# RWKV chunk inverse: the first product of each level as 64x64 blocks, one head at a time, the two lanes alternating between the halves of the array

## The reference, cut to what matters

```
def _rwkv7_step(S, inp):
    r_t, w_t, k_t, v_t, kk_t, b_t = inp
    sa = jnp.einsum('bhvk,bhk->bhv', S, -kk_t)
    S = S * w_t[:, :, None, :] + sa[..., None] * b_t[:, :, None, :] + v_t[..., None] * k_t[:, :, None, :]
    y = jnp.einsum('bhvk,bhk->bhv', S, r_t)
    return S, y
```

## Time and profile before

| | us |
|---|---|
| median of 3 runs | 4005.11 (3998.64 to 4005.95) |
| the profiled execution, its own time | 4005.71 |
| its span, first to last instruction | 4003.9 |
| PE busy in the span | 3716.2 (93%) |
| the chunk stage, first to last `lx` | 1157.1 to 1884.3 of the span |

### The profile page before, as it was taken

The page is one execution under the profiler, slowest core; times in us unless marked ns, Lnnn a source line. Parts: engine busy times, 40 slices in busy tenths (PEclk is TensorE's granted clock), DMA queues, the critical chain, the costliest instruction groups (busy, mean ns, idle before and its releaser), DMA issues. The chain is left out here.

```text
span 4003.9 us, 60255 instructions
## 1 busy us (share of the span) xinstructions
PE 3716.2 (93%) x23340; PEld 3513.3 (88%) x23340; DVE 1701.5 (42%) x2728; ACT 1095.0 (27%) x1680; POOL 77.9 (2%) x67
## 2 busy tenths in 40 slices
PE   6999999996659999999799797999999999799899
PEld 6999999995449999999799686999999999778687
DVE  6566622223856666666443445222222222211333
ACT  5211134334633333333311333111111111111211
POOL 0000000000010000100000000000000000000000
PEclk8999999997779999999899998999999999899999
DMA  5333343343642222221432441111111110311342
GB/s 146 98 117 113 114 143 118 124 126 124 231 134 49 53 58 54 47 54 30 143 114 93 151 138 55 53 52 42 42 42 53 51 42 32 115 51 50 110 124 92
DMA packets 316612, 357.97 MB, mean 89 GB/s; under 512 B 169024, under 2 KB 265152, under 8 KB 304752
## 3 DMA queue, kind: packets, MB, share of 16 engines
q1 hardware_dynamic: 316528, 356.83, 28.5%
HBM read 221.75 MB, written 135.00 MB: 89 GB/s over the span
## 5 line engine op out<-in xcount | busy, mean ns | idle before, releaser
L2225 PE MATMUL psum<-h_hi,up_w_hi 128*128 128x344 f32 x2112 | 676.6, 320 | 15.4 <-DVE up_w_lo L2269 15.4
L2225 PE MATMUL psum<-h_lo,up_w_hi 128*128 128x344 f32 x2112 | 677.6, 321 | 0.0
L2225 PE MATMUL psum<-h_hi,up_w_lo 128*128 128x344 f32 x2112 | 675.4, 320 | 0.0
L434 PE MATMUL psum<-x_hi,proj_w_hi 128*128 128x344 f32 x1632 | 535.0, 328 | 9.4 <-DVE proj_w_lo L521 8.4
L434 PE MATMUL psum<-x_lo,proj_w_hi 128*128 128x344 f32 x1632 | 524.9, 322 | 0.0
L434 PE MATMUL psum<-x_hi,proj_w_lo 128*128 128x344 f32 x1632 | 523.6, 321 | 0.0
L2225 PEld LDWEIGHTS psum<-h_hi,up_w_hi 128*128 128x128 f32 x2112 | 398.3, 189 | 15.5 <-issue 15.5
L2225 PEld LDWEIGHTS psum<-h_hi,up_w_lo 128*128 128x128 f32 x2112 | 398.5, 189 | 0.0
L2225 PEld LDWEIGHTS psum<-h_lo,up_w_hi 128*128 128x128 f32 x2112 | 397.8, 188 | 0.0
L434 PEld LDWEIGHTS psum<-x_hi,proj_w_hi 128*128 128x128 f32 x1632 | 309.3, 189 | 11.1 <-issue 8.5
L2019 PE MATMUL psum<-down_w_hi,down_a_hi 128*128 128x512 f32 x704 | 281.0, 399 | 39.7 <-DVE down_w_lo L2139 29.8
(11 more groups left out here) (305 smaller groups left out, 6236.6 us busy)
## 6 DMA issues: line engine op xcount, KB each, us to landing
up_weight<-in_w_up_tiles SPq DMA_DIRECT2D x22, 1024.0 KB, 4.8
scratch_hidden<-up_hidden SPq DMA_DIRECT2D x22, 1024.0 KB, 3.9
down_a_raw<-scratch_hidden SPq DMA_DIRECT2D x32, 704.0 KB, 5.1
proj_area<-scratch_s_tab SPq DMA_DIRECT2D x32, 608.5 KB, 3.8
scratch_s_tab<-proj_area SPq DMA_DIRECT2D x16, 1089.0 KB, 4.3
proj_weight<-in_w_in_tiles SPq DMA_DIRECT2D x34, 512.0 KB, 4.8
scratch_gates<-proj_mixed SPq DMA_DIRECT2D x16, 1032.0 KB, 4.4
scratch_rwkv_proj<-proj_mixed SPq DMA_DIRECT2D x14, 1032.0 KB, 6.2
```

The costliest lines, as they stand in the source:

```text
L434: mm = nc.tensor.matmul(psum[:, bank(v, n), 0:N_TOK], w[:, v, k, :], x[:, k, cols], start=(k == 0 and w is w_hi and x is x_hi), stop=(k == ...
L2225: mm = nc.tensor.matmul(psum[:, bank(u, part, n), 0:N_TOK], w[:, u, part, k, :], y[:, k, block_cols(n)], start=(k == 0 and w is w_hi and y ...
```

## The change

In each level, the first product is made for both lanes together instead of lane after lane. TensorE first waits for the inputs of both lanes, and then adds to a new semaphore `lx_begun`, for which nothing waits. Each matmul of 128x128 becomes two of 64x64, one for each head: the weights are the head's block of `l_t` (rows and columns of the head), the moving operand is 64 columns of `x` on the head's 64 partitions, and the result goes to the head's 64 partitions and 64 columns of the bank. The two blocks outside the diagonal are no longer written; they keep what the bank held, and the mask multiplies them by zero. In the order, lane 0 on one head alternates with lane 1 on the other: lane 0 head 0 pair 0, lane 1 head 1 pair 0, and so on over the pairs, then the same with the heads exchanged. The last matmul of each lane tells VectorE of it. Everything else stands as before.

```
@@ -1177,15 +1177,29 @@
-            def lx(lane, v, k, l):
+            def lx_inputs(lane, v, k, l):
                 if l == 0:
                     at(pe, x1_ready[lane], 1, k, 1)
                 else:
                     at(pe, x_ready[lane], LEVELS, k, l)
                     at(pe, xt_ready[lane], LEVELS - 1, k, l)
-                for j in range(PAIRS):
-                    mm = T_.matmul(bank(LX[lane])[:, j, :], l_t[:, lane, j, :], x[:, lane, j, :], start=True, stop=True)
-                mm.then_inc(lx_done[lane], 1)
+
+            def one_head(out, weights, moving, lane, j, h):
+
+                rows, block_ = slice(h * S, (h + 1) * S), slice(h * S, (h + 1) * S)
+                return T_.matmul(bank(out[lane])[rows, j, block_], weights[rows, lane, j, block_], moving[rows, lane, j, block_], start=True, stop=True)
+
+            def lx(place, l):
+                for lane in place:
+                    lx_inputs(*place[lane], l)
+                pe.sem_inc(lx_begun, 1)
+                for other in range(2):
+                    for j in range(PAIRS):
+                        for lane in place:
+                            h = other if lane == 0 else 1 - other
+                            mm = one_head(LX, l_t, x, lane, j, h)
+                            if other == 1 and j == PAIRS - 1:
+                                mm.then_inc(lx_done[lane], 1)
@@ -1297,7 +1311,9 @@
                     for chain in (lx, xq, turn_x):
-                        if l < count - 1 or chain is not turn_x:
+                        if chain is lx:
+                            lx(place, l)
+                        elif l < count - 1 or chain is not turn_x:
                             for lane in place:
```

More of the change, by code:

```diff
@@ L1009, in rwkv_chunks @@
     GROUPS = (NC_ + 1) // LANES
-    (masks_loaded, pre_loaded, a_loaded, r_loaded, cleared, bkv_cleared, main_cleared, late_cleared, grams_cleared, eps_set) = sems(name, [
-        "masks_loaded", ("pre_loaded", LANES), ("a_loaded", 4), ("r_loaded", 4), "cleared", "bkv_cleared", "main_cleared", "late_cleared", "grams_cleared", "eps_set"])
+    (masks_loaded, pre_loaded, a_loaded, r_loaded, lx_begun, cleared, bkv_cleared, main_cleared, late_cleared, grams_cleared, eps_set) = sems(name, [
+        "masks_loaded", ("pre_loaded", LANES), ("a_loaded", 4), ("r_loaded", 4), "lx_begun", "cleared", "bkv_cleared", "main_cleared", "late_cleared", "grams_cleared", "eps_set"])
     (grams_done, masked, q_init, toks_done, toks_ready, x1_turned, x1_ready, lx_done, q_ready, xq_done, x_ready, xt_turned, xt_ready) = sems(name + "_pre", [
```

## The result

| | us |
|---|---|
| before, median of 5 runs | 4000.38 (3998.64 to 4005.95) |
| changed, median of 5 runs | 4014.14 (4008.63 to 4022.21) |
| ratio, changed to before | 1.0033, 95% interval 1.0017 to 1.0049 |
| the profiled execution of the changed kernel, and its span | 4018.77, 4017.0 |

The span is 13.1 us longer than that of before.

A forecast was written before the change was run, and what follows sets the result against it. TensorE, busy 713.6 of 730 us in the chunk stage, was taken as the bound; -9.0 us over 16 groups and +0.6 for the first gave -8.4, so 3997 us, range 3985 to 4035.

The forecast's parts named there:

- rival B: Chunk-stage product: only every second pair of matmuls overlaps, product some 1.4 us deep, +20 us, 4025; chance 0.12.
- C: Chunk-stage product: no overlap, records one after another at 0.06 us, +3.7 us a group, 4066 (4081 at 0.066); chance 0.20.
- Two halves at once: First product: matmuls on different array halves overlap fully, 16 records deep at 0.06 us, 0.96 us.
- The passage between shapes: Into and out of the 64x64 blocks: next load unhidden, 0.20 us after the last record's start, 0.09 of it pause.
- Rival A: Passages to 64x64 and back need no pause and hide their loads: -0.96 us a group, -15 us, 3990; chance 0.10.
- The common wait: Before each product both lanes wait for ScalarE's second copy; first load 0.06 us after it, VectorE's first multiplication starts later.
- The increment of `lx_begun`: One sequencer instruction for each product, costed at nothing; without cover, below 0.05 us x 83.
- The sum for a group: Levels 0 to 4 give 0, +0.05, -0.47, +0.19, -0.33 us: -0.56 us a group, -9.0 us over 16 groups.
- the matmuls double to 32 records: First product of both lanes: 32 records, costed at 0.06 us each, 16 deep if two run at once.
- The first group: One-lane group, no alternation: smaller records and passages of 0.2 us cost +0.6 us over three levels.
- 16 records at 0.06 instead of 8 at 0.112: One-lane group's product: record count and pace in us, part of its +0.6 us over three levels.
- The clock in the stage: Chunk stage: granted clock still 1.00 after the change; a fall to the lower level would make all of this wrong.

The follow-up runs named there:

- the two after it: Changed product in levels 2 and 4 alone, ratio 1.0012 to the kernel before; in level 2 alone, 1.0016; both keep TensorE's two-group loop.

## Why the prediction was wrong, point by point

The forecast was 8.4 us less; the medians say 13.8 us more. That the time lies within the range is luck: the range reached to 4035 for rival B, half an overlap, and B is not what happened. The chance of 0.32 for a slower kernel stood on B and C alone.

- **Two halves at once: right.** 0.030 us a record for both streams together; the forecast had 0.06 in each. Rivals B and C are out. C leaned on the Trainium skill's rule in "TensorE: Matmul & The Clock Gate", part 1, of 62 ns of sequencer time for each matmul without hardware decoding. That case is not this one: 32 matmul records took 1.15 us, not the 1.98 that the prediction had from the rule.
- **The passage between shapes: right.** `xq` and the pieces start where the sum has them. In the changed kernel's level 3 the first load comes at 1523.88, 0.20 after the start of the last record before it, and the next load after the product is 1.11 later than its first, as forecast. Rival A is out: the loads are not hidden.
- **The common wait: right in place, a little off in size.** The load follows the end of ScalarE's second copy by 0.11 us (1509.46 + 1.08 to 1510.65), not 0.06. The increment of `lx_begun`, costed at nothing, is not what makes the difference: with one event instruction that carries both waits and the increment it is 0.07. How the waits are spread over the sequencer's instructions was not in the sum. Where they make two event instructions, as in the written-out kernel, that costs 0.54 us a group, as much as the whole gain. In the loop it cost little and did not turn the result.
- **The sum for a group: right.** -0.56 forecast, 44.55 against 45.12 measured with the loop written out and one event instruction. It is no luck of terms that cancel. From one product's first load to the next (levels 0 to 1, 1 to 2, 2 to 3, 3 to 4, and 4 to 0 of the next group) the forecast's starts and terms ask for -0.15, -0.09, -0.47, +0.34 and -0.19 us; that run against the written-out kernel before has -0.14, -0.08, -0.51, +0.34 and -0.18.
- **The step that failed: "the matmuls double to 32 records", costed as engine time only.** The instructions behind them were counted nowhere. 320 more in a body of 1685 (334 by the trace, with the waits) push TensorE's loop out of its instruction store, the body is fetched again for each iteration, and TensorE waits at the jump back. The line of instruction fetches on the page (55 of 16 KB, 14 of them in a stage whose loop ran seven times) could have shown beforehand that the loop ran from the store, and so that its size was a resource. The sum had this at nothing; it measured +20.2 us over six jumps (some 3 of them by the clock after one stop) against the 9 gained.
- **The first group:** +0.6 us forecast for the one-lane products, +3.9 measured. The step "16 records at 0.06 instead of 8 at 0.112" held the clock to be given. It fell for 14 us, and `xq` and the grams alone were 3.7 us longer by it.
- **The clock in the stage** was to stay 1.00; it did, but for that group and 7 us after one stop.

## What to carry to other kernels

Count a change in instructions as well as in busy time wherever an engine runs a loop: ask how many instructions the body has and whether the page's instruction queue shows that they are fetched once or for each iteration. Smaller matmuls that run side by side are worth their time on two conditions: that the loop body stays small (or is written out), and that their waits stand in a single event instruction. Use them only in those levels where TensorE, and not the answer of another engine, ends last: here two levels of five gave more than all five.

## What the runs showed of the hardware that was not expected

- TensorE's loop of 1685 instructions runs from its store, one of 1751 does not. The passage is abrupt: the branch goes from 0.21 us to 3.5 or more, nine 16 KB fetches come with each iteration, and the engine stands still for 2 to 3 us of it, since it works off its queue at first.
- The jump of a body of 3356 instructions costs no more (3.4 and 3.8 us) than that of one of 1751: it fits this that only the wait for the first line after the jump shows, while straight code is fetched ahead in time (93 fetches and no stop in the kernel before, written out).
- Four waits ahead of one product (two for each lane) became two event instructions 0.11 us apart, and the first load came 0.22 us after the last input instead of 0.07. Leaving out the implied ones ahead of four products a group took it from 45.10 to 44.55 us, and the ratio from 0.9994 (0.9984 to 1.0003) to 0.9978 (0.9967 to 0.9989).
- The granted clock fell to its lower level for 3.4 to 7 us after 8 of the 18 stops of the three kernels with six jumps (1 in the change, 4 and 3 in the two after it), and such a group was 1.4 to 3.4 us longer than one with a stop alone.
- Matmuls of 64x64 on opposite corners of the array, in different banks, keep a pace of 0.030 us a record, 3.7 times that of whole ones, for twice the records.
